# A macaron block with forgetting attention and HGRN2 on one core: v as one block of high and low columns, output groups in two operations

## The reference

```
for blk in range(S // Q_BLOCK):                 # Q_BLOCK = 128
    q0 = blk * Q_BLOCK; L = q0 + Q_BLOCK
    s = einsum('bhqd,bhkd->bhqk', q[:, :, q0:L], k[:, :, :L]) * scale
    s = s + F[:, :, q0:L, None] - F[:, :, None, :L]
    s = where(kpos <= qpos, s, -inf)
    p = softmax(s, axis=-1)
    outs.append(einsum('bhqk,bhkd->bhqd', p, v[:, :, :L]))
```

## Time and profile before

| | |
|---|---|
| time, median of 3 runs | 2147.67 us (2145.52 to 2148.44) |
| time of the profiled execution | 2144.34 us |
| its span, first to last instruction | 2142.6 us |
| busy | PE 97%, PE weight loads 81%, DVE 63%, ACT 40%, POOL 6% |
| mean granted TensorE clock | 0.982 of full |
| the four attentions, from the start of the span | about 794 to 868, 943 to 1019, 1093 to 1169, 1243 to 1319 us |

### The profile page before, as it was taken

One profiled execution on the slowest core, in us unless ns is written; L12 is line 12 of the kernel. 1 busy time (PEld: TensorE's weight loads), 2 busy tenths in 40 slices (PEclk: granted clock), 3 DMA queues, 4 the chain that ended last, 5 costly groups with the idle time before them and its releaser, 6 DMA issues.

```text
span 2142.6 us, 27991 instructions
## 1 busy us (share of the span) xinstructions
PE 2068.1 (97%) x10081; PEld 1731.4 (81%) x10081; DVE 1359.5 (63%) x1903; ACT 849.8 (40%) x1219; POOL 123.2 (6%) x211
## 2 busy tenths in 40 slices
PE   4999999998999999999999999999999999999998
PEld 4888888887888878888887878787888888888787
DVE  6977787765664566666577567748766666643334
ACT  5433333332243365456456456325333333322322
POOL 6000000001100000000000000000000000000000
PEclk7999999999999999989999999999999999999999
DMA  9354454338744411100101010332322333254443
GB/s 364 91 143 118 141 143 134 88 107 304 259 167 147 153 26 30 31 21 21 32 20 31 21 30 23 112 103 79 99 72 75 88 88 88 79 209 144 153 157 122
DMA packets 181918, 230.88 MB, mean 108 GB/s; under 512 B 7508, under 2 KB 137676, under 8 KB 180812
## 3 DMA queue, kind: packets, MB, share of 16 engines
q1 hardware_dynamic: 155300, 132.72, 20.7%
q0 software_dynamic: 23424, 84.16, 11.9%
q10 hardware_dynamic: 3112, 12.86, 1.7%
HBM read 189.59 MB, written 40.11 MB: 107 GB/s over the span
## 4 chain that ended last, share of the span: by engine, by line
PE 85%; DVE 6%; DMA 3%; ACT 3%; issue 2%; SPq 0%; POOL 0%; DVEq 0%; ACTq 0%
PE ps L727 26%; PE ps L729 26%; PE ps L728 26%; PE ps L990 2%; DMA ada_late<-in_w_ada_dram 1%; PE ps L938 1%; PE ps L924 1%; PE ps L742 1%; DMA ada_second<-in_w_ada_dram 1%; PE ps L927 1%; DVE neg_max L1979 1%; ACT probs L1405 1%; ACT pT_hi L1413 1%; PE ps L735 1%; DMA x_rows<-in_x_dram 1%
## 5 line engine op out<-in xcount | busy, mean ns | idle before, releaser
L727 PE MATMUL ps<-h_hi,w_hi 128*128 128x512 f32 x720 | 293.2, 407 | 10.9 <-DVE h_lo L1737 4.8
L729 PE MATMUL ps<-h_hi,w_lo 128*128 128x512 f32 x720 | 286.5, 398 | 0.0
L728 PE MATMUL ps<-h_lo,w_hi 128*128 128x512 f32 x720 | 285.9, 397 | 0.0
L727 PE MATMUL ps<-da_hi,dw_hi 128*128 128x512 f32 x704 | 276.8, 393 | 5.5 <-DVE dw_lo L1841 5.4
L729 PE MATMUL ps<-da_hi,dw_lo 128*128 128x512 f32 x704 | 275.0, 391 | 0.0
L728 PE MATMUL ps<-da_lo,dw_hi 128*128 128x512 f32 x704 | 274.9, 391 | 0.0
L727 PE MATMUL ps<-T_hi,op_hi 128*128 128x512 f32 x640 | 249.4, 390 | 0.0
L729 PE MATMUL ps<-T_hi,op_lo 128*128 128x512 f32 x640 | 249.0, 389 | 0.0
L728 PE MATMUL ps<-T_lo,op_hi 128*128 128x512 f32 x640 | 249.0, 389 | 0.0
L1212 ACT ACTIVATE op_hi<-S_f 128x512 fp32r<-128x512 f32 x160 | 100.8, 632 | 309.6 <-PE ps L729 299.4
L1838 DVE TENSOR_TENSOR da_lo<-act_raw,da_hi 128x512 fp32r<-128x512 f32 x88 | 60.9, 692 | 212.8 <-ACT da_hi L1261 212.8
(11 more groups left out here) (287 smaller groups left out, 3594.6 us busy)
## 6 DMA issues: line engine op xcount, KB each, us to landing
w_raw<-in_ffn_w_out_dram POOLq DMA_DIRECT2D x84, 512.0 KB, 3.7
raw<-in_ffn_w_in_dram SPq DMA_DIRECT2D x44, 512.0 KB, 5.4
raw_odd<-in_ffn_w_in_dram SPq DMA_DIRECT2D x44, 512.0 KB, 5.8
act_rows<-act_out SPq DMA_DIRECT2D x44, 512.0 KB, 3.4
act_raw<-act_rows SPq DMA_DIRECT2D x88, 256.0 KB, 2.6
ada_ring<-in_w_ada_dram POOLq DMA_DIRECT2D x32, 512.0 KB, 3.9
raw<-in_w_in_mix_dram SPq DMA_DIRECT2D x29, 512.0 KB, 3.9
ada_late<-in_w_ada_dram POOLq DMA_DIRECT2D x24, 512.0 KB, 4.7
```

The source lines that it names most:

```text
L727: pe.matmul(dst, whi, mhi, start=start, stop=False)
L728: pe.matmul(dst, whi, mlo, start=False, stop=False)
L729: return pe.matmul(dst, wlo, mhi, start=False, stop=stop)
```

## The change

v's parts are stored per head: for each block of 128 tokens and each head e, 64 columns of the high part followed by the 64 columns of the low part of that head. One block of 128 stationary columns then holds both parts, and the product needs two matmuls in place of three: this block by the high and by the low part of the probabilities. The result has the high part's sum in PSUM rows 0 to 63 and the low part's in rows 64 to 127. (So low by low is now added, which was left out before.) `out_group` therefore has two DVE operations: a copy of rows 64 to 127 into `mixed`, a wait for it on DVE's own semaphore, and an addition of rows 0 to 63. `t_O` counts two per group.

In DVE's order, `out_group(g)` moves from the end of step 2g + 3 to step 2g + 4, between that step's row maximum and its reciprocal; groups 6 and 7 stand in steps 16 and 17 behind the last `pT_lo_tile`. `round_lo(3)` moves from step 12 to 13, and the gate's multiplication of `kk` from step 10 to 11.

```diff
-        v_hi, v_lo = ov("v_hi", [P, TT, P], F32R, 16), ov("v_lo", [P, TT, P], F32R, 20)
+        v_st = ov("v_st", [P, TT, 2, 2, HD], F32R, 16)
...
                 if g >= 2:
-                    pe.wait_ge(t_O, TT * i + g - 1)
+                    pe.wait_ge(t_O, 2 * (TT * i + g - 1))
                 for kb in range(jg + 2):
                     c0 = P if kb == jg + 1 else 0
-                    last = three_pass(ps[:, 3, g % 2, c0:2 * P], v_hi[:, kb], v_lo[:, kb], pT_hi[:, kb, c0:2 * P],
-                                      pT_lo[:, kb, c0:2 * P], kb == 0, kb == jg + 1)
+                    v_both = v_st[:, kb, g // (TT // 2)].rearrange("p s k -> p (s k)")
+                    dst = ps[:, 3, g % 2, c0:2 * P]
+                    pe.matmul(dst, v_both, pT_hi[:, kb, c0:2 * P], start=kb == 0, stop=False)
+                    last = pe.matmul(dst, v_both, pT_lo[:, kb, c0:2 * P], start=False, stop=kb == jg + 1)
                 last.then_inc(t_PV, 1)
...
-                pe.wait_ge(t_O, TT * (i + 1))
+                pe.wait_ge(t_O, 2 * TT * (i + 1))
...
-                act.activation(v_hi[:, :, :].rearrange("p t k -> p (t k)"), pair(1), ACT.Copy).then_inc(a_vhi, 1)
+                act.activation(v_st[:, :, :, 0, :], pair(1).rearrange("p (t e k) -> p t e k", e=2, k=HD), ACT.Copy).then_inc(a_vhi, 1)
...
                 dve.wait_ge(t_PV, TT * i + g + 1)
-                dve.tensor_copy(mixed[r, i, jg * P:(jg + 2) * P], ps[r, 3, g % 2, 0:2 * P]).then_inc(t_O, 1)
+                dst = mixed[r, i, jg * P:(jg + 2) * P]
+                dve.tensor_copy(dst, ps[HD:P, 3, g % 2, 0:2 * P]).then_inc(t_O, 1)
+                dve.wait_ge(t_O, 2 * (TT * i + g) + 1)
+                dve.tensor_tensor(dst, ps[0:HD, 3, g % 2, 0:2 * P], dst, ALU.add).then_inc(t_O, 1)
...
-                if n == 10:
+                if n == 11:
                     dve.wait_ge(g_sig, 4 * i + 2)
                     dve.tensor_scalar(kk[:, :], kk[:, :], one_less_lb[:, bass.ds(i, 1)], None, ALU.mult
                                       ).then_inc(g_gates, 1)
...
-                        if n in (2, 7, 12):
-                            round_lo(i, {2: 1, 7: 2, 12: 3}[n])
+                        if n in (2, 7, 13):
+                            round_lo(i, {2: 1, 7: 2, 13: 3}[n])
+                        if n >= 4 and n % 2 == 0:
+                            out_group(i, n // 2 - 2)
                         gate_step(i, n)
                         scale_probs(i, n)
...
-                    if n >= 3 and n % 2 == 1:
-                        out_group(i, (n - 3) // 2)
-                    if n == 16:
+                    if n >= 2 * TT:
+                        out_group(i, n - 10)
+                    if n == 2 * TT:
...
-                dve.tensor_tensor(v_lo[:, :, :].rearrange("p t k -> p (t k)"), pair(1),
-                                  v_hi[:, :, :].rearrange("p t k -> p (t k)").bitcast(F32), ALU.subtract).then_inc(a_vlo, 1)
+                dve.tensor_tensor(v_st[:, :, :, 1, :], pair(1).rearrange("p (t e k) -> p t e k", e=2, k=HD),
+                                  v_st[:, :, :, 0, :].bitcast(F32), ALU.subtract).then_inc(a_vlo, 1)
```

## The result

The changed kernel takes 2126.8 us (median of 4 runs, 2125.38 to 2127.88) against 2148.06 for the kernel before (4 runs beside them); the ratio is 0.9912 with a 95% interval of 0.9895 to 0.9928. The profiled execution has 2125.9 us against 2144.34: 18.4 less.

The account below looks back on a forecast made before the run. PE was taken as the bound, 85% of the chain that ended last, with waits for exponentials. Savings followed along PE gave 4.55 us a round, 18.2 us for four: 2147.67 - 18.2 = 2129.5 us, range 2121.5 to 2138.5.

Parts of the forecast that it names:

- The steps of the sum: Savings followed along PE from wait to wait through one attention round: 4.55 us a round, 18.2 us for four.
- Group 3's saving: 0.93 us of products, expected to become a PE wait before the scores of step 10.
- ACT's idle time that closes in step 10: Idle time on ACT in step 10 expected to vanish, estimated at 0.1 us, adding to the shift by step 12.
- the wait of step 13: PE's wait of 0.29 us in step 13, expected to go and bring the shift to 3.2 us.
- Cost of the added sum zero: DVE's second operation per output group, about 0.42 us, expected to be hidden in DVE's idle time.
- Taking the copy off the path: Output-group copy leaves the chain before the row maximum, which starts 0.33 us earlier; bounds 0 and 0.41.
- the 1.7 us for a held sum: Behind the last group, the sum might wait for POOL: 0.42 us a round, 1.7 us for four at most.
- (a): Rival: PE waits more, no gain from the copy's move or groups 3 and 4; 10.9 us gain, 2136.8; chance 0.14.
- (b): Rival: ACT does not hold steps 10 and 12; 6.04 us a round, 24.2 in all, 2123.5; chance 0.14.
- (c): Rival: added idle before steps 10 and 12 halves the clock until step 16; 22 us slower, 2169.5; chance 0.03.
- (d): Milder clock rival: hgrn's low clock goes away or comes in one more round, 4.6 us either way; inside forecast's 0.65.
- hgrn unchanged: Sign of being right: the hgrn stretches stay as before while an attention gets some 4.5 us shorter.

Follow-up runs that it names:

- e4: Changed kernel with one triple of filler more in steps 9 and 11, one less in steps 16 and 17; 2122.32 us, ratio 0.9882.
- e5: Changed kernel with one sigmoid less on ACT in step 8, kk made by DVE in step 9 as one minus the forget value; ratio 0.9882.
- e3: Changed kernel without the added sum, the low part's rows left out of the output; 2130.78 us, ratio 0.9927.
- e2: Kernel before with DVE's new order only: three products, v's old layout, one copy per output group; ratio 0.9994.
- e11: Repeat of e2, the kernel before with DVE's new order only; ratio 0.9994.
- e1: Changed kernel with DVE's old order: two products and v's new layout, both output operations before the next row maximum; 2144.73 us, ratio 0.9998.
- e6: Changed kernel with PE's hardware loop over rounds 1 to 3 written out; 2124.05 us, ratio 0.9900.

## Why the prediction was right

**The time.** 2129.5 was forecast, 18.2 us under the kernel's 2147.67. The first visit gave 2126.8, 21.3 less than the kernel before beside it; the second gave 2130.57, 14.1 less. The attentions, of which the sum speaks, gave 19.6. The profiled execution was forecast at 2126.1 and has 2125.9. That close it is by luck, since one stretch of hgrn alone differs by 3 us from one execution to the next, and a part of the median's nearness is luck for the same reason.

**The products.** 320 matmuls in place of 480. Group 1 of round 1 in the changed kernel, its first product, its first over 128 columns, and what follows it:

```profile
958.26 0.28 PE L954 MATMUL ps<-pT_hi,v_st 128*128 128x256 f32 x1
...
958.98 0.22 PE L954 MATMUL ps<-pT_hi,v_st 128*128 128x128 f32 x1
...
959.15 0.73 PE L938 MATMUL ps<-ident,probs 128*128 128x128 f32 x5
```

Six products over 256 columns take 0.72 us, 0.12 each, the pitch of before; the two over 128 columns take 0.17, 0.085 each, where three had taken 0.29. The group is shorter by 0.47 us (0.89 for 1.36), forecast 0.45. PE's busy time in an attention falls from 68.2 to 63.2 us.

**The steps of the sum.** Shift of each place in rounds 1 to 3, forecast and measured against the scores of step 1: step 7, 1.18 and 1.23 to 1.28; step 9, 2.20 and 2.28 to 2.34; step 10, 2.20 and 2.27 to 2.33; step 12, 2.9 and 3.06 to 3.16; step 13, 3.2 and 3.56 to 3.69; the end, 4.55 and 5.00 to 5.12. Group 3's saving was lost in step 10, to 0.01 us; e4 and e5 show that ACT's list was the reason. A part of group 4's was lost in step 12.

Three terms were too small. The products gave 4.7 us a round and not 4.58: from the start of a group to the next instruction, groups of 2, 4, 6 and 8 blocks take 0.41, 0.89, 1.37 and 1.85 us, before 0.64, 1.35, 2.08 and 2.80. ACT's idle time that closes in step 10, an estimate of 0.1, was 0.2: exp(9) ends 2.27 to 2.33 us earlier than before, exp(11) 2.48 to 2.55. And the wait of step 13, read as 0.29 from the earlier trace rows, gave 0.50 to 0.53. A bracket at a matmul counts from the end that is shown for the one before, while a matmul that does not wait starts 0.24 us before that end, so the whole wait is 0.24 more than the bracket. With the three the round comes to 4.55 + 0.1 + 0.1 + 0.24 = 5.0. (Step 11 gave 0.65 to 0.69 for a bracket of 0.43 in the same way, but this wait stood in no term, since ACT's list decides when the scores of step 12 start.) The new waits before steps 10 and 12 were forecast as 0.9 and 0.7; with 0.24 added to their brackets they are 0.98 and 0.83.

**The output groups.** Cost of the added sum zero: right, in every step (e3). Taking the copy off the path, 0.33 us in each step: right (e2 and e11: 1.7 to 1.8 us in each of rounds 1 to 3, 1.4 expected; 0.9 and 1.3 in round 0). What the prediction did not say, and should have, is that the two parts need each other. Alone they shorten the attentions by 3.1 and 6.1 us, together by 19.6. The expectation of e1 has it, but it was written after the result, and a reader of the sum alone could think that 18.3 us of products and 5 us of order add up separately.

**POOL.** The timeline behind the last group of round 1:

```profile
1009.23 1.89 POOL L713 TENSOR_TENSOR A<-z_b 128x1024 f32<-128x1024 f32 x1 [140.72 <-PE ps L955]
...
1009.76 0.42 DVE L2006 TENSOR_TENSOR mixed<-ps,mixed 64x256 f32 x1
...
1010.25 1.96 DVE L2090 TENSOR_TENSOR dec<-z_b 128x1024 f32<-128x1024 f32 x1
```

The sum runs its usual 0.42 us in the middle of POOL's instruction. The next operation, with both inputs in SBUF, starts 0.46 us later than it did before, counted from the last group's end, and ends 1.1 us after POOL all the same. In all four rounds of both kernels it ends 3.06 us after the last group. So the sum costs nothing here either, and the 1.7 us for a held sum were not needed. SBUF — State Buffer in the Trainium skill, in its section "Who interferes with whom", has the rule that a DVE instruction with at most one SBUF input, outside the modes that use both port pairs, does not contend with GpSimd. The trace agrees for this operation, which has one input in PSUM and one in SBUF: 0.42 us inside POOL's 1.89.

**The rivals.** (a), 10.9 us in all, is out by the attentions. (b) is out in steps 10 and 12, and e5 shows a part of what it would have brought, 3.5 us of its 6. (c), a low clock in the attention, is out: the granted clock is 0.99 in round 0 and 1.00 in the others, with new waits of 0.74 and 0.59 us in it. Its argument from the earlier trace rows was misread twice: the waits there are 0.3 to 0.8 us and not 0.5 to 0.8, and the 0.97 comes from the time before step 1, since from step 1 on that attention has 1.00. TensorE: Matmul & The Clock Gate in the Trainium skill, under "A second HAM failure mode", warns of frequent micro-idles between groups of matmuls. e1, with 4.8 us of them in a round of 69 us, kept 0.99 to 1.00 there. (d) was the right worry and sized too small: in the prediction it was 4.6 us either way, and the stretches of hgrn in the two profiles of the changed kernel differ by 6.6.

**hgrn unchanged**, as I had put it, holds for the work and its order and not for its length.

## What to carry to other kernels

A product taken off the busiest engine is worth its time only as far as the chain that feeds that engine's next wait gets shorter too: list the waits that the busy engine already has, put the new work of the other engines in their idle time and not in front of the next link, and follow the saving from wait to wait. Where another engine's own list holds a link (here ACT's table loads), the saving turns into idle time, and filler work can be moved into it for nothing. And where one stretch of a kernel varies by several us between executions, judge an edit by the stretch that it touches, and the whole by repeated runs and their mean clock.

## What the runs showed that was not expected

The granted clock in hgrn decides over more time than most of these edits. In the 14 profiles it falls to half for 3 to 7 us at a time, and each profile has another selection of the falls. Three places come again, some 44 to 48, 54 to 61 and 71 to 79 us after the end of an attention's last group. The first has a fall in about half of the 42 stretches, the second in a quarter, the third in all but three. A fourth place, 2 to 4 us after that end, has six. The first place in round 0 of the kernel before, in its chain of waits in time order:

```profile
909.92 1.68 PE ps L742 x16
911.60 1.84 PE ps L990 x16
...
914.41 0.43 PE ps L727
```

and the stretches on either side of the fall, with the granted clock (columns as above):

```profile
910.00:913.00 3.00, 3.00 (x29) 3.00 (x29) 1.90 (x5) 1.78 (x3) 0.00 (x0) 1.00 0.20 59
914.00:917.00 3.00, 3.00 (x8) 2.33 (x8) 0.00 (x0) 2.97 (x4) 0.00 (x0) 0.50 0.00 0
```

Before the fall PE had no idle time, but it did 16 products of two columns (L742) and 16 of 64 columns (L990) for 3.5 us. Then the filler's pitch is 0.43 us, where it had been 0.23: 1.2 GHz in place of 2.4. The second place lies behind the same kind of work, without idle time too.

The third place is different. It lies at the end of hgrn, where PE has waited 1.32 us for ACT and then does 16 products of one column:

```profile
1091.29 1.95 PE L742 MATMUL ps<-ones,dec 128*128 128x1 f32 x16 [1.32 <-ACT dec L1557]
```

The fourth is the loop's jump. The changed kernel's first profile has a fall there, behind the idle time of 2.02 us (the row at 1011.17 under e6):

```profile
1012.00:1015.00 3.00, 3.00 (x9) 2.21 (x9) 3.00 (x4) 2.76 (x4) 1.07 (x3) 0.50 0.10 22
```

In the ten versions and repeats that keep PE's loop, the jump comes 20 times. The six falls came behind 1.89 to 2.49 us of idle time (twice in e3 and e4, once in e1 and the changed kernel), and the other 14 times the idle time was 1.16 to 1.87 us. The versions with the loop written out have none. In e1's attention waits of up to 1.3 us brought no fall. So idle time went ahead of some falls and short products in a row of others. That the short products cause them was not tried, nor what decides in which execution a fall happens, nor why all versions but the kernel before tend to a lower mean clock in their timed runs (0.977 to 0.981, against 0.981 to 0.982 in its 78 runs).
